# One more wait on SyncE: the second unit's expert weights are issued after the first unit's tokens have landed

## Chip, cores and metric

The kernel runs on one core of one Trainium2 chip. The metric is the device time of one execution in microseconds (us); lower is better. Engines are named TensorE (PE in the profile; PEld is its weight load), VectorE (DVE), ScalarE (ACT), GpSimd (POOL) and SyncE (SP). SP and POOL issue the DMAs that matter here.

## What is computed

One layer of a hybrid backbone for 384 tokens of width 1024 (128 context tokens and 256 latent tokens): a modulated norm, a token mixer (chunked gated linear attention beside low-rank attention), a gated residual, a second modulated norm, and a mixture of 64 experts with one shared expert. The change stands in the mixture of experts:

```python
scores = jax.nn.sigmoid((t @ lp['w_router']).astype(jnp.float32))
...                                     # group-limited choice of 8 of 64 experts
gates = jnp.sum(jax.nn.one_hot(top_e, N_EXPERTS, dtype=jnp.float32) * w[..., None], axis=-2)
def block(args):
    tb, gb = args
    a = jax.nn.silu(jnp.einsum('td,edf->tef', tb, lp['w_exp_gate'])) * jnp.einsum('td,edf->tef', tb, lp['w_exp_up'])
    a = a * gb[:, :, None].astype(a.dtype)
    return jnp.einsum('tef,efd->td', a, lp['w_exp_down'])
shared = (jax.nn.silu(t @ lp['w_sh_gate']) * (t @ lp['w_sh_up'])) @ lp['w_sh_down']
```

All is float32. Each expert has a gate and an up matrix of 1024 x 256 and a down matrix of 256 x 1024.

## The kernel before

Every engine has one program, written out in order, and engines wait for each other by semaphores. Up to about 230 us the kernel computes the mixer and the second norm. Then come the routing tables (VectorE, with small matmuls on TensorE), beside which TensorE computes the shared expert, and then the experts.

The experts run in **units** of 128 token slots, two experts to a unit, and two units make a **pair** (a unit is a half of its pair, `half` 0 or 1). The routing tables say which token stands in which slot and which experts a unit has (`jobs`). Experts 0 and 1 are always in unit 0 (`PINNED`), so their weights are loaded without waiting for the tables. For each unit TensorE does, in this order: `up` (64 matmuls of the tokens `xs` with `raw_gu`), a scatter of the unit before, `turn`, the rest of that scatter, and `down` (32 matmuls with `raw_dn`). Between the two `down`s of a pair it turns the tokens of the next pair (`tokens_t`, line 1029), both halves.

The weights lie in two sets of buffers, `raw_gu[half][j]` and `raw_dn[half][j]`. SyncE loads the weights of unit u + 2 when unit u has used its own: gate and up together as one load of 2 MB for each expert (`load_gu`, semaphore `gu_in[half]`), down as one load of 1 MB (`load_dn`, semaphore `dn_in[half]`). Unit 1's weights are the first that wait for the table `jobs`; SyncE issues them in this order: gate/up of its first expert, down of both, then, once the shared expert has freed the buffer and POOL has begun, gate/up of its second expert.

The tokens are brought in by POOL. The rows of the second norm's result are spilled to `h2_dram`, and an indirect DMA gathers 128 rows of 4 KB (or fewer, empty slots move nothing) into `xg[half]`, semaphore `xg_in[half]`. There is one gather for unit 0 (line 2150, as soon as VectorE has written `slot_row` at line 1873), one for unit 1 (line 2155), and two for each later pair (line 2141), issued when VectorE has the pair's slot rows and TensorE has turned the pair before. TensorE's wait for the first gather is `pe.wait_ge(xg_in[0], 16)` at line 1104, behind all of the shared expert's up matmuls.

Before TensorE may start a unit's `up` it waits for `gated`. VectorE gives the first count of it at line 1961 by an increment of its own, after the table of overflow owners (lines 1931 to 1939):

```python
V.scalar_tensor_tensor(offs[0:NE], offs[0:NE], cap[0:NE], owner[0:NE], ...).then_inc(S["owner_ready"], 1)
...
dve.sem_inc(S["gated"], 1)
take_slots(0)
tokens(0, 0, 2)
```

Of the kernel before, what the change touches and what calls it, by code (L numbers as in the profile page):

```python
# [126 lines left out]
def build(nc, A, O):  # L127

    ctx = ExitStack()
    with ctx:  # L130
# [5 lines left out]
        def sem(name):  # L136
            return ctx.enter_context(nc.semaphore(name))
# [56 lines left out]
        for n, (_, w) in CW.items():  # L194
            if n not in KEEP + LATE:
                TCW[n] = (o, w)
                o += w
# [150 lines left out]
        xg_in = [sem(f"xg_in{k}") for k in range(2)]  # L348
# [58 lines left out]
        def _(sp):  # L407
# [79 lines left out]
            def load_gu(half, experts, js=(0, 1)):  # L487
                for j in js:
                    sp.dma_start(raw_gu[half][j][:], gate_up_of(experts[j])).then_inc(gu_in[half], 16)
# [5 lines left out]
            def gate_up_of(e):  # L495
                return A["c_gate_up"][e].rearrange("p (c n) -> p c n", c=NC)
# [4 lines left out]
            def experts_of(unit, js=(0, 1)):  # L501

                return [sp.value_load(jobs[0:1, bass.ds(unit * 2 + j, 1)] if not isinstance(unit, int)
                                      else jobs[0:1, unit * 2 + j:unit * 2 + j + 1], min_val=0, max_val=NE - 1) for j in js]
# [15 lines left out]
            sp.dma_start(w_shd[:], A["w_sh_down"][0].rearrange("(p c) n -> p c n", c=2)).then_inc(S["shd_in"], 16)  # L520
            sp.wait_ge(S["jobs_ready"], 1)
            second = experts_of(1, (0,))
            load_gu(1, second, (0,))
            second += experts_of(1, (1,))
            load_dn(1, second)
# [1684 lines left out]
```

## Time and profile before

| | us |
|---|---|
| median of 3 executions | 765.43 |
| lowest and highest | 763.59, 765.44 |
| span of the profiled execution (first to last instruction) | 761.5 |
| TensorE busy in the span | 738.5 |
| VectorE busy | 391.2 |
| ScalarE busy | 136.6 |
| POOL busy | 50.3 |

The profiled execution's own time is known by its span; the timed executions are 2 to 4 us longer than that span, which is what lies around the first and the last instruction. The granted TensorE clock is at full speed over the whole span. The DMA engines are busy in nearly all of the second half and move 268.79 MB, 353 GB/s on the mean. Busy time of TensorE comes from modelled ends of matmuls, so the share says that it has work without a break, not that it works at its peak.

### The profile page before, as it was taken

How to read it: one execution, taken by the hardware profiler on the slowest of the kernel's cores; microseconds unless marked ns; L12 is line 12 of the kernel's file. 1: busy time of each engine (PE TensorE's matmuls, PEld its weight loads, DVE VectorE, ACT ScalarE, POOL GpSimd, SP SyncE). 2: the span in 40 equal slices, each digit the busy share in tenths (PEclk: the TensorE clock that was granted, in tenths of full speed). 3: DMA queues.
4: the chain of work that ended last, by engine and by line, in shares of the span. 5: the costliest groups of instructions: out<-in, count | busy, mean ns of one | idle time of the engine just before them, and what ended most of it. 6: DMA issues, size and time to landing. Idle time of an engine off the chain costs nothing.

```text
span 761.5 us, 13554 instructions
## 1 busy us (share of the span) xinstructions
PE 738.5 (97%) x5035; PEld 348.9 (46%) x5035; DVE 391.2 (51%) x876; ACT 136.6 (18%) x287; POOL 50.3 (7%) x52
## 2 busy tenths in 40 slices
PE   4999999989999899999999999999999999999998
PEld 1554434566555443444435354444453444435433
DVE  2236486574786444445436354443454445435557
ACT  3124010421211121111211111111111111211120
POOL 0000000101000011101010010100101101011000
PEclk9999999999999999999999999999999999999999
DMA  9994468181728899999999999999999999999992
GB/s 338 386 391 167 166 217 338 67 318 39 303 83 326 361 412 423 424 420 422 429 425 425 413 422 430 418 425 423 420 422 426 426 421 423 428 425 423 423 388 83
DMA packets 41087, 268.79 MB, mean 353 GB/s; under 512 B 5308, under 2 KB 7996, under 8 KB 21984
## 3 DMA queue, kind: packets, MB, share of 16 engines
q1 hardware_dynamic: 36448, 255.77, 82.3%
q0 software_dynamic: 4608, 12.59, 4.2%
q8 instruction: 21, 0.34, 0.2%
q14 instruction: 10, 0.08, 0.0%
HBM read 269.01 MB, written 3.52 MB: 358 GB/s over the span
## 4 chain that ended last, share of the span: by engine, by line
PE 90%; DVE 5%; DMA 3%; issue 1%; SPq 0%; ACT 0%; POOL 0%; POOLq 0%; DVEq 0%; ACTq 0%
PE ps L561 83%; PE ps L1029 4%; DMA xg<-h_spill,slot_row 2%; DMA ada<-in_w_ada 1%; PE ps L1056 1%; PE ps L638 0%; PE ps L843 0%; DVE keyT L1596 0%; DVE stateP L1696 0%; DVE x L1728 0%; PE ps L877 0%; SPq L423 0%; DVE xtmp L1726 0%; PE ps L787 0%; SPq L409 0%
## 5 line engine op out<-in xcount | busy, mean ns | idle before, releaser
L561 PE MATMUL ps<-raw_gu,xs 128*32 128x512 f32 x2048 | 225.9, 593 | 0.6 <-DVEq L1961 0.6
L561 PEld LDWEIGHTS ps<-raw_gu,xs 128*32 128x32 f32 x2048 | 65.4, 110 | 144.8 <-issue 144.6
L561 PE MATMUL ps<-raw_dn,ast 128*32 128x512 f32 x1024 | 116.5, 595 | 0.0
L1958 DVE SCALAR_TENSOR_TENSOR act_a<-ps,small,sil 128x256 f32<-128x256 f32 x32 | 15.5, 484 | 179.1 <-ACT sil L1359 179.1
L1982 DVE TENSOR_TENSOR acc<-acc,ps 128x512 f32<-128x512 f32 x174 | 106.3, 679 | 0.0
L561 PE MATMUL ps<-ys,place 128*128 128x512 f32 x360 | 98.8, 411 | 0.0
L561 PEld LDWEIGHTS ps<-ys,place 128*128 128x128 f32 x360 | 63.3, 189 | 36.0 <-issue 25.1
L1975 DVE TENSOR_TENSOR ys<-ps,ys 128x512 fp32r<-128x512 f32 x60 | 41.5, 692 | 63.2 <-ACT ys L1372 63.2
L2141 POOL DMA_INDIRECT xg<-h_spill,slot_row x30 | 34.2, 1141 | 408.7 <-DVE slot_row L1912 404.1
L561 PEld LDWEIGHTS ps<-raw_dn,ast 128*32 128x32 f32 x1024 | 30.0, 109 | 65.0 <-issue 63.2
L1372 ACT CAST ys<-ps 128x512 fp32r<-128x512 f32 x60 | 35.2, 586 | 104.3 <-PE ps L561 104.3
L1359 ACT ACTIVATE sil<-ps 128x256 f32<-128x256 f32 x32 | 12.3, 385 | 224.0 <-PE ps L561 224.0
L561 PE MATMUL ps<-w_out,mixedT 128*128 128x512 f32 x96 | 43.1, 595 | 1.1 <-issue 1.1
L1029 PE MATMUL ps<-keep,xg 128*128 128x128 f32 x256 | 35.8, 287 | 2.0 <-DMA xg<-h_spill,slot_row 2.0
L1029 PEld LDWEIGHTS ps<-keep,xg 128*128 128x128 f32 x256 | 33.3, 193 | 5.7 <-DMA xg<-h_spill,slot_row 1.4
L561 PEld LDWEIGHTS ps<-w_out,mixedT 128*128 128x128 f32 x96 | 17.5, 190 | 19.6 <-issue 19.5
L1951 DVE COPY xs<-ps 128x512 f32<-128x512 f32 x32 | 22.0, 687 | 5.1 <-PE ps L1029 4.8
L1377 ACT COPY xs<-ps 128x512 f32<-128x512 f32 x32 | 18.8, 587 | 30.2 <-PE ps L1029 30.2
L561 PE MATMUL ps<-w_shgu,h2T 128*128 128x512 f32 x48 | 21.9, 599 | 0.0
L561 PE MATMUL ps<-hT,w_qk 128*128 128x384 f32 x64 | 21.8, 491 | 0.0
L561 PE MATMUL ps<-w_g,hT 128*128 128x512 f32 x48 | 21.5, 597 | 0.0
L561 PE MATMUL ps<-w_v,hT 128*128 128x512 f32 x48 | 21.4, 599 | 0.0
(321 smaller groups left out, 634.3 us busy)
## 6 DMA issues: line engine op xcount, KB each, us to landing
raw_gu<-in_c_gate_up SPq DMA_DIRECT2D x64, 2048.0 KB, 14.2
raw_dn<-in_w_exp_down SPq DMA_DIRECT2D x64, 1024.0 KB, 13.6
ada<-in_w_ada SPq DMA_DIRECT2D x16, 512.0 KB, 11.3
ada2a<-in_w_ada SPq DMA_DIRECT2D x8, 1024.0 KB, 5.2
ada2b<-in_w_ada SPq DMA_DIRECT2D x8, 1024.0 KB, 5.6
w_out<-in_w_out SPq DMA_DIRECT2D x2, 2048.0 KB, 8.5
w_qk<-in_w_in SPq DMA_DIRECT2D x2, 1024.0 KB, 14.8
w_v<-in_w_in SPq DMA_DIRECT2D x1, 2048.0 KB, 13.5
```

The source lines that it names most:

```text
L561: return nc.tensor.matmul(out, l, r, start=first, stop=last)
L1029: last = nc.tensor.transpose(ps[:, bank, c * P:(c + 1) * P], xg[:, half, 4 * n + c::NC], ident)
L1056: last = nc.tensor.transpose(ps[:, 3, f * P:(f + 1) * P], act_a[:, f::2], ident)
L1359: nc.scalar.activation(sil[:], ps[:, 0, 0:DE], ACT.Silu).then_inc(S["silu_done"], 1)
L1372: nc.scalar.copy(ys[:, 0, n * 512:(n + 1) * 512], ps[:, 1 + n, :]).then_inc(S["yh_done"], 1)
L1377: nc.scalar.copy(xs[:, 0:4, half * P:(half + 1) * P], ps[:, 4 + 2 * half, :].rearrange("p (c s) -> p c s", c=4))\
L1951: V.tensor_copy(xs[:, 4:8, half * P:(half + 1) * P], ps[:, bank or 5 + 2 * half, :].rearrange("p (c s) -> p c s", c=4))\
L1958: V.scalar_tensor_tensor(act_a[:], ps[:, 0, DE:2 * DE], gslot[:, half:half + 1], sil[:], ALU.mult, ALU.mult)\
L1975: V.tensor_tensor(ys[:, 1, h], ps[:, 1 + n, :], ys[:].bitcast(F32)[:, 0, h], ALU.subtract).then_inc(S["yl_done"], 1)
L1982: V.tensor_tensor(a, a, ps[:, 4 + (6 * half + k) % 4, :], ALU.add).then_inc(S["acc_done"], 1)
L2141: G.indirect_dma_start(xg[:, half], None, h2_dram, bass.IndirectOffsetOnAxis(ap=slot_row[:, half:half + 1], axis=0), bounds_check=TOK - 1, ...
```

## The change

SyncE waits for `xg_in[0]`, the landing of unit 0's gathered tokens, between reading the number of unit 1's first expert and issuing that expert's gate/up load. All that SyncE issues later stands behind this wait.

```diff
@@ -520,6 +520,7 @@
             sp.dma_start(w_shd[:], A["w_sh_down"][0].rearrange("(p c) n -> p c n", c=2)).then_inc(S["shd_in"], 16)
             sp.wait_ge(S["jobs_ready"], 1)
             second = experts_of(1, (0,))
+            sp.wait_ge(xg_in[0], 16)
             load_gu(1, second, (0,))
             second += experts_of(1, (1,))
             load_dn(1, second)
```

No engine's instructions change place. On SyncE, between the table `jobs` and the loads of unit 1, stands before (`raw_gu_133` and `raw_gu_134` are unit 1's gate/up buffers, `raw_dn_137` and `raw_dn_138` its down buffers):

```order
L503 TENSOR_LOAD jobs [waits jobs_ready]
L503 ISA x2
L489 ISA
L489 DMA raw_gu_133<-in_c_gate_up 128x4096
L503 TENSOR_LOAD jobs
L503 ISA x2
L493 ISA
L493 DMA raw_dn_137<-in_w_exp_down 128x2048
L493 ISA
L493 DMA raw_dn_138<-in_w_exp_down 128x2048
L489 ISA [waits begun,wo_done]
L489 DMA raw_gu_134<-in_c_gate_up 128x4096
```

And the same place on SyncE with the change:

```order
L503 TENSOR_LOAD jobs [waits jobs_ready]
L503 ISA x2
L489 ISA [waits xg_in0]
L489 DMA raw_gu_133<-in_c_gate_up 128x4096
L503 TENSOR_LOAD jobs
L503 ISA x2
L493 ISA
L493 DMA raw_dn_137<-in_w_exp_down 128x2048
```

The first load of unit 1 has got the wait; the rows behind it are as they were. Lines of the kernel from 523 on are numbered one higher after the change.

## Rows read from the trace of the kernel before

**Rows 1.** The page: the span, and each engine's busy time, share and instructions.
```profile
span 761.5 us, 13554 instructions
...
PE 738.5 (97%) x5035; PEld 348.9 (46%) x5035; DVE 391.2 (51%) x876; ACT 136.6 (18%) x287; POOL 50.3 (7%) x52
```

**Rows 2.** Chain that ended last, 240 to 320 us: start, us, what.
```profile
257.50 0.04 DVE rt L1939
...
257.79 7.11 PE ps L561 x64
...
270.46 13.10 DMA xg<-h_spill,slot_row
...
283.61 1.16 PE ps L1029 x8
```

**Rows 3.** Timeline of all engines, 254 to 258.2 us: start, us, instruction, [idle before, releaser].
```profile
256.09 1.13 PE L1029 MATMUL ps<-keep,xg 128*128 128x128 f32 x8 [0.83 <-DMA xg<-h_spill,slot_row]
...
257.79 0.64 PE L561 MATMUL ps<-raw_gu,xs 128*32 128x512 f32 x4 [0.57 <-DVEq L1961]
```

**Rows 4.** Timeline of SyncE's DMA issues, 225 to 300 us.
```profile
244.88 0.35 SPq L489 DMA_DIRECT2D raw_gu<-in_c_gate_up  x1
246.00 0.90 SPq L493 DMA_DIRECT2D raw_dn<-in_w_exp_down  x2
254.84 11.08 SPq L489 DMA_DIRECT2D raw_gu<-in_c_gate_up  x3
```

**Rows 5.** Timeline of POOL, 225 to 320 us.
```profile
246.72 1.20 POOL L2150 DMA_INDIRECT xg<-h_spill,slot_row  x1 [41.50 <-DVE slot_row L1873]
255.97 0.99 POOL L2155 DMA_INDIRECT xg<-h_spill,slot_row  x1 [8.05 <-DVE slot_row L1924]
268.93 1.23 POOL L2141 DMA_INDIRECT xg<-h_spill,slot_row  x1 [11.97 <-DVE slot_row L1912]
```

**Rows 6.** Tile xg: issue to landing of the gather issued at 246.72.
```profile
DMA to landing us min/median/max: 9.2/9.2/9.2
```

**Rows 7.** Tile xg: issue to landing of the gather issued at 255.97.
```profile
DMA to landing us min/median/max: 9.6/9.6/9.6
```

**Rows 8.** Windows: busy us of each engine (instructions), clock, DMA share, GB/s.
```profile
263.00:264.00 1.00, 1.00 (x16) 0.41 (x12) 0.00 (x0) 0.00 (x0) 0.00 (x0) 1.00 0.34 131
264.00:266.00 2.00, 1.42 (x13) 0.43 (x4) 0.66 (x2) 0.76 (x2) 0.00 (x0) 1.00 0.04 16
266.00:268.00 2.00, 2.00 (x20) 1.91 (x24) 1.38 (x4) 0.96 (x2) 0.00 (x0) 1.00 1.08 311
268.00:273.00 5.00, 5.00 (x52) 1.48 (x48) 2.86 (x9) 1.17 (x2) 2.22 (x2) 1.00 1.01 429
```

**Rows 9.** DMA queues, 247 to 251 us (q1: SyncE's): packets, MB, share.
```profile
q1 hardware_dynamic: 95, 1.56, 92.4%
```

**Rows 10.** DMA queues, 251 to 255 us (q0: POOL's gathers).
```profile
q1 hardware_dynamic: 172, 1.34, 79.4%
q0 software_dynamic: 142, 0.32, 20.6%
```

**Rows 11.** DMA queues, 269 to 273 us (there is no q0 row).
```profile
q1 hardware_dynamic: 120, 1.72, 101.4%
```

**Rows 12.** DMA queues, 273 to 277 us.
```profile
q1 hardware_dynamic: 85, 1.38, 80.3%
q0 software_dynamic: 79, 0.32, 19.6%
```

**Rows 13.** Timeline of TensorE, 262 to 286 us.
```profile
265.88 0.50 PE L1056 MATMUL ps<-keep,act_a 128*128 128x128 f32 x2 [0.58 <-DVE act_a L1958]
...
271.23 7.05 PE L561 MATMUL ps<-raw_gu,xs 128*32 128x512 f32 x64
...
281.36 1.05 PE L1029 MATMUL ps<-keep,xg 128*128 128x128 f32 x8
```

**Rows 14.** Tile raw_dn: issue to landing of the load issued at 379.46.
```profile
DMA to landing us min/median/max: 14.4/14.4/14.4
```

**Rows 15.** Timeline of TensorE, 375 to 398 us.
```profile
393.62 4.90 PE L561 MATMUL ps<-raw_gu,xs 128*32 128x512 f32 x44
```

## Prediction

> **What bounds the kernel now.** I read the page first: TensorE is busy 738.5 of 761.5 us [rows 1], so a microsecond lost by TensorE ahead of the long row of expert units is a microsecond of the kernel, and one gained on another engine is nothing. Then the chain that ended last, for the stretch where SyncE issues the second unit's weights [rows 2]. It shows two things. Ahead of the first expert matmuls (257.79) the chain stands on VectorE, which works on the table of overflow owners until 257.5; the gather of the first unit's tokens is not in it. And between 270.46 and 283.61 the chain is one piece of 13.10 us: the gather of pair 1's second half. TensorE had finished the first half's turns at 281.36 + 1.05 = 282.4 [rows 13] and stood until 283.61, so 1.2 us.
>
> Next the timeline just ahead of the first unit [rows 3]. TensorE does wait 0.83 us for the first gather and turns at 256.09, but then it waits another 0.57 us at 257.79, released by VectorE's queue at line 1961. So the first wait has cover: whatever it gives back is lost again at 257.79.
>
> Last the DMA side. SyncE issues unit 1's first gate/up load (2.1 MB) at 244.88, its two down loads (1 MB each) from 246.00 and its other gate/up load at 254.84; that last row also holds the pair for unit 2, the last of it issued by 254.84 + 11.08 = 265.9 [rows 4]. POOL issues the gathers at 246.72, 255.97 and 268.93 [rows 5] and, by the chain, 270.46; I call them A, B, C, D. A lands 9.2 us after its issue, at 255.9 [rows 6], B 9.6 us after, at 265.6 [rows 7]. The DMA queues run nearly empty in 263 to 264 (131 GB/s), stand still from 264 to 266 (16 GB/s), start again at 311 GB/s and then run at 429 GB/s [rows 8]. TensorE needs unit 1's gate/up weights at 271.23 [rows 13].
>
> **The change, part by part.**
>
> *The wait itself* issues nothing; it makes the load of 244.88 wait for A. Queued behind it on SyncE are the two down loads, the load of 254.84 and everything later.
>
> *When does A land if the queues are empty?* No row shows a lone gather. From A's own packets: none moves from 247 to 251 [rows 9], and 142 move from 251 to 255 [rows 10], so the first comes about 4.3 us after the issue. C does the same: issued at 268.93, no gather packet until 273 [rows 11], then 79 in 273 to 277 [rows 12], so at least 4.1 us. A's four quiet microseconds had 1.56 MB of weights beside them and C's 1.72 MB, and those of A began on a queue that had just started; the delay is the same, so I take it as fixed and not as time in a queue. Then the data: 0.32 MB [rows 10] is 0.75 us at 429 GB/s; with the slow start that [rows 8] shows from 266 I take 1.2. From last packet to landing A took 255.9 − 255.0 = 0.9. So A lands at 246.72 + 4.4 + 1.2 + 0.9 = 253.2. Bounds: if the 4.3 us were queueing and the data came right behind POOL's own 1.20 us [rows 5], 246.72 + 1.2 + 1.2 + 0.9 = 250.0; if nothing got quicker, 255.9 as now.
>
> The Trainium skill, "DMA: Bandwidth & Descriptors", section "Anatomy of one DMA", gives a DMA issued from GpSimd about 2.0 us plus its bytes at 436 GB/s. Counted from the end of POOL's instruction that is an estimated 250.7 for A, and the sum below would fall from +2.2 to about +1.0 us; the rows of packets speak against it, and I go by them.
>
> *Gain of the earlier A*: at most the 0.83 us at 256.09, and it is covered by VectorE at 257.79. I cost it at 0. Without that cover it would be −0.8.
>
> *Cost of the later weights.* SyncE now issues the first load at about 253.3 instead of 244.88, 8.4 us later. The down loads follow 1.1 us behind as now, the last load at 255.4 instead of 254.84. The same bytes follow without A's 0.32 MB, which takes 0.75 us off. The stream that ended at 263.3 ends at 263.3 + 8.4 − 0.75 = 270.95. With 0.9 us to landing, unit 1's gate/up is there at 271.85, and TensorE asks for it at 271.23: a new wait of 0.6 us. The pause from 264 to 266 is filled with late weights, and unit 2's pair starts to move at 270.95 instead of 266.
>
> *What that does to C and D*, where it reaches the end. From 273 to 277, 79 gather packets went beside 85 weight packets [rows 12]; from 251 to 255, 142 beside 172 [rows 10]: nearly one for one. The weight packets are 1.38 MB / 85 = 16 KB in the first (gate/up) and 1.34 MB / 172 = 8 KB in the second (down). So a gather's time depends on which weights stand beside it. One engine of 16 moves 429 / 16 = 26.8 GB/s: 0.61 us for a 16 KB packet, 0.31 us for an 8 KB one. C and D have about 9 packets each per engine (142 / 16), 18 in all. Before: by 273.3 unit 2's pair (4.19 MB) had moved 2 × 0.311 + 5 × 0.429 = 2.77 MB [rows 8] and 0.13 more; 1.29 MB were left, 4.9 packets per engine. So 5 of the 18 gather packets went beside large packets and 13 beside small ones. After: the pair has moved only from 270.95 to 273.3, 1.0 MB; 3.18 MB are left, 12.1 packets. So 7.2 more gather packets sit beside large ones, at 0.31 us each: D lands 2.2 us later, at 285.8. TensorE, even 0.6 us late from 271.23, asks for D at 283.0; the 0.6 us vanish in D's wait, which grows from 1.2 to about 2.8.
>
> The Trainium skill, same page, section "Queues, rings and completion order", says that each DMA engine takes turns between queues packet by packet. The rows agree; by that rule A was never behind the whole 4 MB, and it speaks against holding them back.
>
> *B* is issued at 255.97 as now and moves from 260.3, when the down loads are in the queue; A beside down weights took 9.2. So B lands at 265.2 to 266, and TensorE turned it behind the unit's own turns at 265.88 + 0.50 = 266.4 [rows 13]: no wait, or some tenths that D's wait takes up.
>
> *Later pairs*: TensorE's work is unchanged and shifts by D's delay. The weight stream is some 4 us later, 2 us more than TensorE. The tightest place I find is pair 4: a down load issued at 379.46 lands 14.4 us later, at 393.9 [rows 14]. The gate/up pair ahead of it was therefore in by about 391.4 (1 MB at 429 GB/s is 2.4 us), and TensorE asks for it at 393.62 [rows 15]: 2.2 us of slack, just enough. I cost it at 0.
>
> **Sum**: 0 + 0 + 2.2 = +2.2 us on the profiled execution's span of 761.5 us. The executions timed are 763.59, 765.44 and 765.43; 2 to 4 us lie around the span, which the change doesn't touch. So 765.43 + 2.2 = 767.6.
>
> Each microsecond in A's landing moves 0.43 MB, 1.6 packets, 0.5 us of D. A at 250.0 gives +0.6; A at 255.9 gives +3.6.
>
> **Rivals.**
>
> *A lands early (250 to 251.7).* For: the 4.3 us may be partly the queue, since every gather here had weights beside it. Against: A's and C's delays are equal. D is then 0.6 to 1.5 us later: 766.0 to 766.9. Within 0.3%.
>
> *The weights themselves become the wait.* If A lands at 254.9 or later, unit 1's gate/up comes at 273.5 or later, TensorE stands 2.3 us or more at 271.23, D comes 3 to 3.6 us late, and the weight stream uses up the slack at 393.62. +3.1 to +4.3: 768.5 to 769.7. For: that slack is thin. Against: a lone gather would have to be hardly faster than one beside weights.
>
> *Faster.* The first up matmuls start when A is turned and not when VectorE is through. The place is 257.79, the price −0.83; if moreover D found the queue no fuller, up to 1.2 of its wait would go too: 763.4 to 764.6. It decides if VectorE reaches line 1961 before 257.2. Against: VectorE's last rows before 257.5 wait for no DMA, and nothing takes bytes off the queue ahead of D.
>
> *No effect* (the wait is met anyway) is excluded: A lands 11 us after the load's issue.
>
> **How the numbers follow.** The likeliest, 1.5 to 3.0 us slower (A from 251.7 to 254.9), has 0.50: 766.9 to 768.4. A early: 0.22. Weights as the wait: 0.20. Faster: 0.08. The range goes from 764.9, which leaves the faster case outside, to 769.3, which leaves the end of the late case outside. A measurement of this kernel tells 0.3%, 2.3 us, so the border (767.7) lies inside the likeliest case. Slower: 0.23 of it and the late case, 0.43. Faster by over 0.3% (below 763.1) would need the faster case and luck: 0.04. Within: 0.53.
>
> **What would show it.** In the trace of after: SyncE's gate/up load at 253.3 ± 1 with A's landing just ahead of it; TensorE's first turns at about 255.3 with no DMA wait, but the first up matmuls still at 257.8, released by VectorE; no DMA pause between 264 and 266; a wait of some tenths for raw_gu at 271; D landing 15 us after its issue instead of 13.1, and TensorE's wait ahead of the second half's turns about 2.8 us; everything later shifted by 2 us. I am wrong if a lone gather's first packet comes much sooner than 4 us, if gather packets don't go one for one with weight packets, or if the first up matmuls move.

## The result, and the profile after

The change made the kernel a little slower: 765.87 us (median of 20 executions, 764.46 to 767.76) against 764.14 us before (20 executions, 762.79 to 766.07), run in turns on one chip. The ratio is 1.002, its 95% interval 1.0012 to 1.0028. So +1.7 us between the medians where +2.2 was forecast (+1.5 between the means, 764.31 and 765.84). The 20 executions before lie 1.3 us lower than the three whose times stood ahead of the prediction, which brings the forecast time (767.6) too high by as much. The profiled execution of after took 765.05 us with a span of 762.9; wherever both are on record, an execution's time and span lie 2.0 to 2.3 us apart, so the "2 to 4 us" of the prediction compared executions of different length with one span.

The page of after, its span and busy times, for [rows 1]:

```profile
span 762.9 us, 13554 instructions
...
PE 738.7 (97%) x5035; PEld 348.8 (46%) x5035; DVE 391.1 (51%) x876; ACT 136.4 (18%) x287; POOL 50.2 (7%) x52
```

TensorE's work is the same; the span is 1.4 us longer, 0.3 of it ahead of the table `jobs` (written at 243.63 before and 243.93 after), where the change touches nothing. That front part differs from execution to execution of one kernel (243.6 to 247.4 over all traces). To compare traces I therefore take what lies from the start of `jobs` to the end of the span and call it the **tail**: 517.9 us before, 519.0 after. 1.1 us to account for.

SyncE's issues, for [rows 4], and POOL's, for [rows 5], from their timelines in 225 to 320 us:

```profile
251.00 0.35 SPq L489 DMA_DIRECT2D raw_gu<-in_c_gate_up  x1
252.11 0.89 SPq L493 DMA_DIRECT2D raw_dn<-in_w_exp_down  x2
255.13 11.08 SPq L489 DMA_DIRECT2D raw_gu<-in_c_gate_up  x3
...
247.01 1.19 POOL L2151 DMA_INDIRECT xg<-h_spill,slot_row  x1 [41.49 <-DVE slot_row L1874]
```

The load is issued at 251.0, 6 us later than before and not 8.4. The first gather (A) lands 3.8 us after its issue (9.2 in [rows 6]), at 250.8, by the tile's row:

```profile
DMA to landing us min/median/max: 3.8/3.8/3.8
```

The DMA queues from 249 to 250 us, for [rows 9, 10]; it is the only queue that moves:

```profile
q0 software_dynamic: 81, 0.25, 83.7%
```

Seven gather packets fall in 248 to 249, 81 in 249 to 250 and 56 in the next microsecond. With nothing beside it the gather has its first packet 1.9 us after the issue, not 4.3. The Trainium skill, "DMA: Bandwidth & Descriptors", section "Anatomy of one DMA", gives about 2.0 us plus the bytes at 436 GB/s, which was an estimated 250.7 in the prediction. Counted in the same way from the end of POOL's instruction here (248.20) it is an estimated 250.9; the trace agrees (250.8). The case that the prediction took as its rival, A landing at 250 to 251.7, is what happened.

Windows of 4 us (columns as in [rows 8]), where before the same three read 401, 135 and 373 GB/s:

```profile
250.00:254.00 4.00, 4.00 (x14) 1.95 (x13) 1.84 (x4) 0.00 (x0) 0.00 (x0) 1.00 0.58 167
...
262.00:266.00 4.00, 3.59 (x34) 1.20 (x26) 0.37 (x1) 0.75 (x2) 0.00 (x0) 1.00 1.05 442
266.00:270.00 4.00, 3.83 (x36) 2.55 (x40) 3.25 (x9) 0.96 (x3) 0.78 (x1) 1.00 0.99 422
```

Some of the bytes that didn't move while the load was held move in 262 to 266, which was the pause (1.2 MB more than before, and 0.2 MB more in 266 to 270). From there on the queues are as full as before, 424 and 423 GB/s in 300 to 500 us, so the rest of the delay stays.

TensorE's timeline, for [rows 3, 13] and the chain of [rows 2]: the turns of A, the first up matmuls, unit 1's up, pair 1's turns, and the last gate/up wait of the kernel:

```profile
255.40 1.06 PE L1030 MATMUL ps<-keep,xg 128*128 128x128 f32 x8
258.08 7.07 PE L562 MATMUL ps<-raw_gu,xs 128*32 128x512 f32 x64 [1.62 <-DVEq L1962]
...
271.52 7.05 PE L562 MATMUL ps<-raw_gu,xs 128*32 128x512 f32 x64
...
281.65 1.05 PE L1030 MATMUL ps<-keep,xg 128*128 128x128 f32 x8
284.15 1.16 PE L1030 MATMUL ps<-keep,xg 128*128 128x128 f32 x8 [1.45 <-DMA xg<-h_spill,slot_row]
...
740.15 7.07 PE L562 MATMUL ps<-raw_gu,xs 128*32 128x512 f32 x64 [0.56 <-DMA raw_gu<-in_c_gate_up]
```

A's wait is gone and the pause behind it has grown from 0.57 to 1.62 us: the first up matmuls start 14.16 us after `jobs` before and 14.15 after. D's wait has grown by a quarter of a microsecond. Then the new thing: at 740.15 TensorE waits for gate/up weights. At the same place before it went on without a wait (738.75). The chain of after, 690 to 763 us, has a DMA piece there; the chain before had none:

```profile
717.78 22.32 DMA raw_gu<-in_c_gate_up
...
740.15 9.13 PE ps L562 x72
```

In differences to the span before: 0.30 us at `jobs`, 0.29 at the first up, 0.54 at D's turns (284.15 against 283.61), 0.43 at 689.6, 1.40 at 740.15. So of the tail's 1.1 us, +0.25 come at D and +0.97 behind 690 us, with 0.11 given back between. The 0.97 are two late loads. The matmuls of 740.15 lose 0.74 against before. Those of 709.98 lose 0.20: they show no wait of their own, but TensorE's weight load ahead of them does, and before it had none. TensorE's weight loads, 708 to 712 us:

```profile
709.98 0.16 PEld L562 LDWEIGHTS ps<-raw_gu,xs 128*32 128x32 f32 x8 [0.92 <-DMA raw_gu<-in_c_gate_up]
```

The page's DMA rows show the same lag: a gate/up load takes a median of 15.4 us to land, before 14.2; a down load 14.8, before 13.6. How little is left at the end can be read off the gate/up pair that TensorE asks for at 725. Tile raw_gu, the pair issued at 702.95 before, and the pair issued at 703.39 after:

```profile
DMA to landing us min/median/max: 15.3/17.5/19.6
...
DMA to landing us min/median/max: 16.8/19.1/21.4
```

The second load of the pair is issued 0.5 us behind the first. So the pair is in at 723.1 before and 725.3 after, and TensorE asks for it at 725.10 and 725.76: a margin of 2.0 us before and 0.5 after. The same reading of the fourteen gate/up pairs from 296 to 703 us whose landing the traces give (one unit of each pair of units) has the margin 0.7 to 1.8 us smaller after than before in every one. The lag isn't made good anywhere.

### The profile page after: what moved, and what is told of

Same layout as the page of the kernel before. It is cut to its first block, busy times and chain, and to the rows that moved or that the text cites. A ratio compares the mean times of both kernels' runs of the same rounds, so it can differ in the third digit from the quotient of the medians.

```text
span 762.9 us, 13554 instructions
## 1 busy us (share of the span) xinstructions
PE 738.7 (97%) x5035; PEld 348.8 (46%) x5035; DVE 391.1 (51%) x876; ACT 136.4 (18%) x287; POOL 50.2 (7%) x52
## 4 chain that ended last, share of the span: by engine, by line
PE 87%; DMA 6%; DVE 5%; issue 1%; SPq 1%; ACT 0%; POOL 0%; POOLq 0%; DVEq 0%; ACTq 0%
PE ps L562 80%; PE ps L1030 4%; DMA raw_gu<-in_c_gate_up 3%; DMA xg<-h_spill,slot_row 2%; DMA ada<-in_w_ada 1%; PE ps L1057 1%; PE ps L639 0%; PE ps L844 0%; DVE keyT L1597 0%; DVE stateP L1697 0%; DVE x L1729 0%; PE ps L878 0%; DVE xtmp L1727 0%; SPq L423 0%; PE ps L788 0%
## 5 line engine op out<-in xcount | busy, mean ns | idle before, releaser
L562 PE MATMUL ps<-ada,small 128*2 128x256 f32 x128 | 11.5, 469 | 10.3 <-DMA ada<-in_w_ada 10.3
## 6 DMA issues: line engine op xcount, KB each, us to landing
raw_gu<-in_c_gate_up SPq DMA_DIRECT2D x64, 2048.0 KB, 15.4
raw_dn<-in_w_exp_down SPq DMA_DIRECT2D x64, 1024.0 KB, 14.8
w_v<-in_w_in SPq DMA_DIRECT2D x1, 2048.0 KB, 13.6
```

The lines of the kernel that those rows point to most:

```text
L562: return nc.tensor.matmul(out, l, r, start=first, stop=last)
```

## Experiments

Each kernel ran five rounds in turn with the kernel before; ratios are to the kernel before in the same batch and follow the means, so they can differ by some tenths of a microsecond from the difference of the medians (medians 764.18, 764.54, 764.09 and 764.51 us in the four batches). The expectations name three theories. **Stream**: what costs is that the weight stream starts later and has no pause left to make it up, so TensorE meets it wherever it is thin, above all at the end. **Gather**: what costs is D behind larger packets. **Clock**, formed after the first batch: TensorE's longer pauses are followed, in some executions, by a stretch at half the granted clock.

### Release the load earlier or later

The wait for `xg_in[0]` is exchanged for one that is met when POOL has begun on A:

```diff
+            sp.wait_ge(S["begun"], 1)
             load_gu(1, second, (0,))
```

> The hold of unit 1's weights is shortened: SyncE waits until POOL has issued gather A (about 248.3 us) and not until A has landed. Theory S (stream): from the first load on, the weights run without a pause to the end of the kernel, and TensorE meets the stream again at the last gate/up load; a delay costs what is left of it after the pause of 263.3 to 266.1 has been filled, less a few tenths of slack at the end. Here the issue is 3.4 us later than before, the pause and the slow start behind it take back about 3.4: 0.0 to +0.4 us against before, and the pause is nearly gone. Theory G (gather): only the gather that ends TensorE's wait at 284 counts, by large and small packets beside it: +0.1 to +0.5 us. Beside that, of the first gather: if its first packet comes late because weight packets are queued ahead of it, it comes about 1.9 us after the issue here and A lands within 5 to 6 us; if the late first packet needs only weights that run beside it, it is 4.3 us again.

765.35 us (12 executions), ratio 1.0021 (1.001 to 1.0031), tail 518.6. The load went out at 247.25 and A at 247.28; A then landed 10.6 us later, and TensorE stood longer than in the kernel before:

```profile
257.97 1.13 PE L1030 MATMUL ps<-keep,xg 128*128 128x128 f32 x8 [2.15 <-DMA xg<-h_spill,slot_row]
```

So the first up matmuls start 15.23 us after `jobs` and not 14.16; 0.4 us of that is taken back at D, where TensorE waits 0.82 us. There is no wait for gate/up weights. Both theories had this kernel at most 0.5 us slower and it is 1.2 slower by the medians: neither had reckoned with a later A, and 6 of the 12 executions had a mean granted clock of 0.998 or less (see below).

By the theory of packets queued ahead I had expected A in 5 to 6 us. A load issued in the same moment delays the gather no less than one that has been running for 2 us. The numbers together (3.8 alone, 10.6 and 9.2 with weights) show that the 4.3 quiet microseconds come with the traffic beside it and aren't fixed.

Later still, until unit 1's slot rows are written:

```diff
+            sp.wait_ge(S["row_ready"], 1)
             load_gu(1, second, (0,))
```

> The hold is made longer: SyncE waits for VectorE's second slot row (about 255.1 us), 10.3 us later than before, 4.2 us later than with the change. Theory S: unit 1's stream ends 10.3 - 0.75 us later, 3.4 are taken back by the pause, so it is 6.1 us late; TensorE stands about 2 us at unit 1's up matmuls and again later; in all +5.3 to +6.3 us against before. Theory G: the gather ends 2.5 to 3.3 us late, and nothing later costs: +2.5 to +3.3 us. If the cost of the change were a matter of the wait's place and not of its length, it would be +1.7 as there.

770.1 us (6 executions), ratio 1.0073 (1.0058 to 1.0087), tail 523.5, 5.6 us more than before. The load went out at 256.47, and A, alone again, landed 3.7 us after its issue. TensorE waited 2.85 us for gate/up at unit 1's up, and 0.30, 0.46 and 0.35 us for gate/up again at 399, 716 and 746 us; D's wait is gone. The stream theory had +5.3 to +6.3, the gather theory +2.5 to +3.3. The median is +5.9. In the profiled execution 1.7 of the 5.6 us are something else: the up matmuls behind the wait of 2.85 took 8.76 us and not 7.07, at a lower granted clock. The two executions at full clock (769.13 and 770.93 us) are as long as the four others, so the clock doesn't explain the time; six executions are few.

### Give the stream its time back

A down buffer holds two rows of 1024 numbers in each partition. In SyncE's second loop (from pair 7, for the units of pair 8 and later) each down load now brings only the first of the two, 0.5 MB in place of 1 MB; the sums of those units then use what the buffers still hold. Once without the change and once with it:

```diff
+            def load_dn_part(half, experts):
+                for j, e in enumerate(experts):
+                    sp.dma_start(raw_dn[half][j][:, 0:1], down_of(e)[:, 0:1]).then_inc(dn_in[half], 16)
...
             with sp.Fori(SPLIT, n_pairs - 1) as p:
-                next_weights(p)
+                next_weights(p, True)
```

> Before, with less weight traffic in the second half: in SyncE's second loop of pairs the down loads bring only the first half of each row (0.5 MB less for each expert), so the later units multiply old values there; arithmetic and order are the same. Theory S: TensorE hardly waits for the stream in before, so this is 0 to 0.6 us faster than before. Theory G: the same as before, within 0.3 us. This is the base for the next one.

> The change, with the same cut of the down loads in the second loop. Theory S: the stream's delay is made good long before the last load, only the longer wait at 284 us is left: +0.2 to +0.6 us against the kernel before with the same cut, and no wait for a gate/up load in the last pair. Theory G, or any cost that is fixed by the time unit 1 is through: the full +1.5 to +1.7 us against it.

Without the change: 764.49 us (11), ratio 1.0000 (0.9991 to 1.0009), tail 517.5. The kernel before gains nothing from fewer bytes late in the run: its stream didn't bind it. With the change: 765.07 us (11), 1.0008 (0.9998 to 1.0018). The change then costs 0.6 us and not 1.7, as the stream theory had it (+0.2 to +0.6; the other had +1.5 to +1.7), and no wait for gate/up weights is left in the trace. The difference of about 1 us is what the trace of after said of the end, but it isn't much more than these intervals allow. The trace of this kernel has a tail of 520.1, though, longer and not shorter. TensorE, 280 to 290 us:

```profile
284.90 1.97 PE L1034 MATMUL ps<-keep,xg 128*128 128x128 f32 x8 [1.87 <-DMA xg<-h_spill,slot_row]
286.80 4.42 PE L566 MATMUL ps<-raw_dn,ast 128*32 128x512 f32 x32
```

and its windows:

```profile
282.00:286.00 4.00, 2.13 (x14) 1.94 (x13) 2.06 (x4) 0.58 (x1) 0.00 (x0) 0.88 1.07 441
286.00:290.00 4.00, 4.00 (x29) 1.35 (x31) 1.19 (x3) 0.94 (x2) 0.00 (x0) 0.70 0.99 416
```

The same turns took 1.97 us where [rows 2] has 1.16, and the down matmuls 4.42 where after had 3.64: 1.6 us more work time. The granted clock is 0.88 and 0.70 where it was 1.00 over the whole span before, so part of the stretch ran at the lower level, 1.2 in place of 2.4 GHz. What stands ahead of it is a TensorE pause of 1.87 us, in D's wait. This led to the clock theory.

### Load the stream more

A copy of 1 MB from HBM to HBM that nobody uses, issued by SyncE between its two loops (some 480 us in) in the kernel before:

```diff
+            sp.dma_start(copy_dram, down_of(0)).then_inc(S["extra"], 16)
             sp.wait_ge(S["tables_ready"], 1)
```

> Before, plus one copy of 1 MB from HBM to HBM that SyncE issues once, between its two loops of pairs (some 480 us in), and that nobody waits for until the end. Theory S (the weight stream runs without a pause to the last gate/up load, and TensorE meets it there): 2.4 us more of stream, less what is unused and less the slack at the end, +1.0 to +2.3 us. Theory G (only the stretch around 284 us counts): 0, within 0.3 us.

766.18 us (11), ratio 1.0021 (1.0012 to 1.003), tail 519.4, 1.5 us more than before. Nothing of the first units is touched, and yet TensorE waits at the end:

```profile
712.15 7.07 PE L564 MATMUL ps<-raw_gu,xs 128*32 128x512 f32 x64 [0.88 <-DMA raw_gu<-in_c_gate_up]
742.14 3.21 PE L564 MATMUL ps<-raw_gu,xs 128*32 128x512 f32 x28 [0.38 <-DMA raw_gu<-in_c_gate_up]
```

A delay of the stream in mid-run isn't recovered either. None of the 11 executions had a mean granted clock of 0.998 or less. Stream, without gather or clock, is enough for a cost of this size.

### Take D's wait away

Unit 1's down matmuls are put between the turns of pair 1's halves, so that TensorE works while D comes:

```diff
                     tokens_t(half, n)
-            down(0, 1, True)
+                if half == 0:
+                    down(0, 1, True)
```

Without the change, with it, and then without the change but with the cut of down loads from pair 7:

> Before, with one thing moved on TensorE: at the first turn of two halves (the 284 us place) unit 1's down matmuls (3.6 us) come between the turns of the first and of the second half, so that gather D has 3.6 us more to land. TensorE's wait of 1.2 us there is gone. Theory S: the time is not gained in full, since the stream is as late as ever at the end: -0.2 to -0.8 us. Theory G: -1.2 us in full. Clock theory (a long enough wait of TensorE at that place is answered by a stretch at half clock in some executions): no execution with a mean clock of 0.998 or less, where before has 2 of 29.

> The change, with the same move on TensorE, so that the later gather D costs TensorE nothing. Against the kernel before with the move: theory S: +1.2 to +1.9 us, the stream's lag, met at the last gate/up loads, where the trace shows waits. Theory G, and the clock theory by itself: 0 to +0.2 us. Clock theory: no stretch at half clock at 285 us.

> Before with the move on TensorE and with the cut of the down loads in the second half (0.5 MB less for each expert, so later units multiply old values). Theory S: now the whole wait is gained, -1.0 to -1.4 us against before, and -0.4 to -1.0 us against the move without the cut. Theory G: the same as the move without the cut.

| kernel | median us (11 each) | ratio (95%) | tail |
|---|---|---|---|
| moved | 763.79 | 0.9996 (0.9986 to 1.0006) | 517.1 |
| moved, with the change | 765.47 | 1.0013 (1.0004 to 1.0022) | 518.9 |
| moved, with the cut | 763.05 | 0.9988 (0.9979 to 0.9997) | 516.9 |

D's wait is gone in all three and the change still costs 1.7 us by the medians, 1.8 in the tails and 1.1 by the means (the moved kernel had two long executions of 11). None of the 11 executions with the change had a mean granted clock of 0.998 or less. So neither D nor the clock is needed for the cost. It moves to where the prediction had seen the tightest place. TensorE, 372 to 412 and 700 to 765 us, of the moved kernel with the change:

```profile
393.95 7.07 PE L562 MATMUL ps<-raw_gu,xs 128*32 128x512 f32 x64 [1.47 <-DMA raw_gu<-in_c_gate_up]
...
739.93 7.07 PE L562 MATMUL ps<-raw_gu,xs 128*32 128x512 f32 x64 [0.56 <-DMA raw_gu<-in_c_gate_up]
```

The first is the up of [rows 15]. A TensorE that is a microsecond ahead meets there the stream that is late. The moved kernel without the change has no wait there, and 0.17 us at its last gate/up load.

### Delay D alone

In the kernel before, the gather of pair 1's second half is held until unit 0 is through:

```diff
                 for half in range(2):
+                    if hold and half:
+                        pool.wait_ge(S["y_done"], 4)
```

> Before, with only gather D held back: POOL issues it after unit 0's last down matmul (about 271.4 us instead of 270.5), pair 1 only, and nothing is changed in the weights. TensorE's wait at 284 us grows from 1.2 to some 1.7 to 2.1 us. Clock theory: 3 to 6 of 12 executions have a mean clock of 0.998 or less, as with the change (8 of 20), and these are about 1.7 us longer than the others. Without the clock theory: the share of such executions stays at before's (4 of 62). In the other executions +0.2 to +0.9 us against before; by theory S less than the wait has grown, since the stream is not later.

> The changed kernel once more, beside the other two on one chip: +1.4 to +2.0 us against before, a quarter to a half of its executions at a mean clock of 0.998 or less.

The first of them was to lengthen D's wait without touching the stream. It didn't: D was issued at 272.64, 1.8 us later behind C's issue than in the kernel before, and landed 10.9 us later, 39.5 us after `jobs` where it was 39.9 in [rows 2]. TensorE waited 0.77 us. 764.22 us (11), ratio 1.0007 (0.9997 to 1.0017), tail 517.5. A gather issued 1.8 us later lost nothing here; why wasn't looked into. On the clock theory the run says little: 2 of its 11 executions had a mean granted clock of 0.998 or less, and in its trace the wait is no longer than before. The second is the changed kernel once more, in the same batch: 765.01 us (11), 1.0016 (1.0007 to 1.0025), tail 518.9; by the medians that is +0.9 us where I had expected +1.4 to +2.0, by the means +1.3. Its D landed 13.95 us after the issue, and TensorE waited 2.04 us there, and its matmuls not at all at the end:

```profile
285.65 1.16 PE L1030 MATMUL ps<-keep,xg 128*128 128x128 f32 x8 [2.04 <-DMA xg<-h_spill,slot_row]
```

So the changed kernel pays about the same in different places in different executions: 1.45 at D and 0.56 at the end in one, 2.04 and nothing in the other.

### Move and cut together

With the change, unit 1's down moved and the down loads cut from pair 7. If stream, D and the end were all, nothing should be left of the cost:

> The change, with the move on TensorE (unit 1's down matmuls ahead of the turns of the second half) and with the cut of the down loads in the second half (so later units multiply old values). Theory S: neither gather D nor the late stream costs anything any more, so it is where the same kernel without the change was, -0.9 to -1.4 us against before (that one had -1.2). If the change costs anything by another way (SyncE's order, the first gather, the first unit), it shows here: -0.6 us or slower.

764.87 us (11), ratio 1.0009 (1.0 to 1.0018), tail 518.4: 0.8 us over the kernel before instead of about 1 under it. Its trace has the half-clock stretch at another place, behind the first pause. TensorE, 255 to 270 us:

```profile
258.97 8.74 PE L566 MATMUL ps<-raw_gu,xs 128*32 128x512 f32 x64 [1.62 <-DVEq L1967]
```

and the window from 250 to 262:

```profile
250.00:262.00 12.00, 10.38 (x52) 5.53 (x54) 5.72 (x19) 1.39 (x4) 0.99 (x1) 0.87 0.82 319
```

64 matmuls in 8.74 us instead of 7.07. That explains the trace and not the median (2 of the 11 executions had a low mean clock), so both kernels of this comparison ran once more, side by side:

> The change with the move and the cut (later units multiply old values), once more. Its trace, counted from the table of jobs to the end, was 518.4 us with a stretch at half clock of 1.7 us in the first up matmuls, so 516.7 without it, and that of the one without the change 516.9; but its median was 2 us above the other's. Theory S: in executions without a low clock the two differ by less than 0.5 us. If something of the change is still unexplained: 1.5 us or more between them again.

> The kernel before with the move on TensorE and the cut of the down loads, once more, beside the same with the change on one chip. -0.9 to -1.4 us against before, as measured the first time.

Without the change 763.4 us (11), 0.9985 (0.9976 to 0.9994), tail 516.8; with it 765.18 us (11), 1.0007 (0.9998 to 1.0016), tail 518.4. The gap is there again, 1.8 us by the medians and 1.5 in the tails, and this time without a half-clock stretch. It is one wait:

```profile
395.24 7.07 PE L566 MATMUL ps<-raw_gu,xs 128*32 128x512 f32 x64 [1.81 <-DMA raw_gu<-in_c_gate_up]
```

The cut begins with pair 7; the late stream is met in pair 4, ahead of it. My expectation had left that place out, though the prediction had named it. The two traces of this one kernel have the same tail, 518.4: one lost 1.7 us at half clock ahead of pair 4 and then found its weights there, the other kept the clock and waited 1.8 us for them. Where the stream is late, what TensorE loses ahead of it is not lost twice.

### Uncover the gain

The prediction said that A's earlier landing is worth nothing because VectorE's table of owners stands ahead of `gated`. So the table is written behind the first token copy, with the change; and, as the version that ought to be best, without the change together with the moved down:

```diff
             dve.sem_inc(S["acc_done"], 6)
+            i = take("start")
+            freed(V.tensor_copy(base[0:NE], i[0:NE, 0:1]))
...
+            V.scalar_tensor_tensor(offs[0:NE], offs[0:NE], cap[0:NE], owner[0:NE], ALU.subtract, ALU.mult).then_inc(S["owner_ready"], 1)
             gated(0, 0)
```

> The change, with VectorE's table of overflow owners moved behind the first unit's token copy, so that line 1961 is reached as soon as the slot row is done: the cover that hid the gain of the earlier gather is gone. The first up matmuls start 0.9 to 1.2 us earlier, counted from the table of jobs. Theory S: no use for the end, since the late stream is met later: +0.3 to +1.3 us against before. If the start of the first unit were what counts: 0.5 us faster than before or better. The pause of TensorE ahead of the first up matmuls is 0.7 us instead of 1.6, so low clock there should be gone.

> Before without the change, with VectorE's table moved behind the first token copy and unit 1's down matmuls moved ahead of the turns of the second half: the version that the experiments point to. The first up matmuls start about 0.3 us earlier, so unit 2's weights are issued earlier and the stream's pause is shorter by as much; D's wait is gone. -0.6 to -1.3 us against before.

With the change: 765.69 us (11), 1.0014 (1.0005 to 1.0023). The first up matmuls now start 12.85 us after `jobs` and not 14.15: with the cover gone the early A gives 1.3 us at this place. At the end nothing of it is left, the tail is 519.7. Unit 1's gate/up comes 0.2 us late, D's wait is 2.06, and behind it the clock falls. TensorE, 252 to 300 us:

```profile
256.78 7.07 PE L562 MATMUL ps<-raw_gu,xs 128*32 128x512 f32 x64 [0.32 <-ACT xs L1378]
...
284.02 1.97 PE L1030 MATMUL ps<-keep,xg 128*128 128x128 f32 x8 [2.06 <-DMA xg<-h_spill,slot_row]
285.93 4.39 PE L562 MATMUL ps<-raw_dn,ast 128*32 128x512 f32 x32
```

and the window from 284 to 288:

```profile
284.00:288.00 4.00, 3.98 (x20) 2.10 (x24) 1.19 (x3) 0.59 (x1) 0.00 (x0) 0.57 1.04 434
```

Without the change: 763.32 us (11), ratio 0.9986 (0.9977 to 0.9995), tail 516.9. This version does all of the reference's work and is 1.1 us faster than the kernel before by the ratio. Its first up starts at 14.22 us after `jobs`, so the moved table gives nothing here (A's wait of 1.14 us takes the place of VectorE; I had expected 0.3 us), and the gain is probably the moved down's, D's wait: the tail is 516.9 where the moved down alone had 517.1. Why the moved down alone gained less by its ratio (0.9996) isn't settled; the two intervals overlap. The end wait is 0.2 us.

## Why the prediction came out as it did

**Right: the gain has cover.** The first up matmuls didn't move (14.16 and 14.15 us behind `jobs`), and with VectorE's table out of the way they moved by 1.3 us. Both sides of that claim are shown.

**Wrong: "the delay is the same, so I take it as fixed and not as time in a queue".** A and C both had weights beside them, so their equal delay could not tell the two apart; I read agreement of two loaded cases as evidence on the unloaded one. Alone, the first packet came after 1.9 us and A landed at 250.8, not 253.2. The stream was held back by 6.1 us and not 8.4.

**Right in mechanism, too large: the cost through C and D.** The pause at 264 to 266 filled up and D's wait grew, from 1.20 us to 1.45, 1.87 and 2.04 in three traces with the change (0.83 to 1.20 in three without it), by less than the 1.6 forecast, and the wait at 271.23 did not come. With A at 250.8 the prediction's own rate (0.5 us of D for each us of A) gives about +1.0, which is near the larger two. The kernels with the moved down show that without D's wait the change costs as much.

**Wrong: "2.2 us of slack, just enough. I cost it at 0".** This is the term that carries the cost. The lag of the stream was taken to be some 2 us against TensorE and to be harmless; but the DMA queues run at about 424 GB/s from here to the last weights, and nothing gives a lag back. TensorE meets it at 393.6 if it is ahead (1.47 and 1.81 us in two kernels), or at the end (0.56 at 740 in the profiled execution; 0.97 us of the tail lie behind 690). The slack was read at the tightest place that I had found and not where the stream has drawn nearest at the end, where the margin was 2.0 us before and 0.5 after. The longer delay (+5.9 us), the extra megabyte (+1.6) and the moved down (+1.7) all agree with it.

**Not foreseen: the clock.** 8 of the 20 executions of the changed kernel had a mean granted clock of 0.998 or less. Their mean is 766.86 us, against 765.16 for the other 12 and 764.31 for the kernel before. So 0.85 us of the +1.5 between the means are there without any low clock, near the 1.1 of the traces, and 8/20 of 1.7 us, 0.7, are the executions with it. Of the kernel before, 4 of 62 executions in the first two batches and 0 of 60 in the last two had a low mean.

The link to TensorE's longer pauses is only argued. For it:

- Five traces show such a stretch, all close behind a TensorE pause: the change with the cut (1.87 us), with the moved down and the cut (1.62), with the moved table (2.06), the release at the slot rows (2.85), and the moved down with the cut but without the change (1.58). The last has it in the mixer, at 156 to 160 us, where nothing was changed.
- Of the executions of kernels in which unit 1's weights are released later than before and its down matmuls stand at their old place, 29 of 71 had a low mean. Of those with the moved down, where D's wait is gone, 7 of 77 had: 3 of 33 with the change and 4 of 44 without.

Against it:

- The changed kernel had it in only 2 of 11 when run again, with 2.04 us at D.
- The pause of 1.6 us ahead of the first up matmuls stands in every kernel with the change except the one with the moved table. The change with the moved down has it, and had no low mean in 11; and the kernel before has a pause of 1.59 us in the mixer and hardly ever a low mean.

The one run meant to isolate it did not lengthen the wait. That stays open.

The total came near by luck. It falls into the case that had the highest chance (1.5 to 3.0 us slower), but that case needed A at 251.7 to 254.9. A came as in the rival case, which was priced at 0.6 to 1.5. Errors of opposite signs did the rest: D and the release too large, the far end and the clock at nothing.

## What to carry to other kernels

Where a DMA stream runs without a pause to the end, what its early pauses don't take back of a later start is never made good. Holding it back to let a small transfer through costs at the place where the consumer comes closest to it (here up to 490 us later), so follow the lag to the last load before costing it at nothing. Before paying for an earlier landing, look at what else the consumer waits for; here VectorE held the same start. And a delay that two loaded transfers share says nothing on how one would do alone.

## What the runs showed of the hardware

- A gather of 0.32 MB landed 3.7 to 3.8 us after its issue alone and 9.2 to 10.6 us after it beside weight loads; its first packet came after 1.9 us in the one case and after 4.3 to 4.6 us in the other, even where the weights were issued in the same moment. Why the first packet waits so long was not settled.
- In some executions, behind pauses of 1.58 to 2.85 us, TensorE ran a few microseconds in which the granted clock of the 4 us windows fell to 0.57 to 0.88 (stretches at 1.2 in place of 2.4 GHz): 32 down matmuls took 4.4 instead of 3.64 us, 64 up matmuls 8.7 instead of 7.07. A stretch cost 1.6 to 1.7 us in these traces, less where TensorE would have waited for late weights later on anyway. What decides in which executions it comes was not settled.
